# Reordering one core's three-block network: first-layer front, attention heads one by one, feed-forward fronts, and GpSimd's queue

## The reference

```
rkv = einsum(xs[:3], w_rkv);  r, k, v = rkv
decay = exp(-exp(w_log));  a = sigmoid(a0 + (xa @ a1) @ a2);  g = sigmoid(xg @ g1) @ g2
kk = (k * k_k) / max(norm(k * k_k), 1e-12)
k = k * (1.0 + (a - 1.0) * k_a)
S_t = S_{t-1} * w_t + (S_{t-1} @ -kk_t) (kk_t * a_t)^T + v_t k_t^T;  y_t = S_t @ r_t
yn = (y - mean) * rsqrt(var + LNX_EPS) * lnx_w + lnx_b
bonus = sum(r * k * r_k) * v;  out = ((yn + bonus) * g) @ w_o
MLA: q, k from latents, 32 of 96 columns rotated; softmax(q k^T + mask) v, 16 heads
conv_ffn: gate, up = x @ w_in;  h = gelu(conv(gate)) * up;  h @ w_out
```

## Time and profile before

| | |
|---|---|
| median of 3 runs | 1089.64 us (1087.91, 1089.64, 1090.89) |
| the profiled execution's own time | 1084.79 us |
| its span | 1083.0 us |
| mean granted clock of TensorE | 0.997 |
| busy: TensorE, VectorE, ScalarE, GpSimd | 1060.6, 791.5, 611.5, 219.0 us |
| chain that ended last | TensorE 77%, VectorE 12%, DMA 3%, issue 2%, ScalarE 2%, GpSimd 2% |

### The profile page before, as it was taken

One profiled execution on the slowest core, in us unless ns is written; L12 is line 12 of the kernel. 1 busy time (PEld: TensorE's weight loads), 2 busy tenths in 40 slices (PEclk: granted clock), 3 DMA queues, 4 the chain that ended last, 5 costly groups with the idle time before them and its releaser, 6 DMA issues.

```text
span 1083.0 us, 18718 instructions
## 1 busy us (share of the span) xinstructions
PE 1060.6 (98%) x7143; PEld 915.8 (85%) x7143; DVE 791.5 (73%) x1092; ACT 611.5 (56%) x965; POOL 219.0 (20%) x234
## 2 busy tenths in 40 slices
PE   7999999999999999999999999999999999999997
PEld 6997798888888898789888888998777889888886
DVE  7997867878885568777888666688868776666543
ACT  6766276656664576855666454645665446555531
POOL 0125483122220011001222100561100001112200
PEclk9999999999999999999999999999999999999999
DMA  8553172657767466455766674556552654666552
GB/s 247 171 174 123 40 231 84 176 156 195 192 195 264 149 146 172 122 134 142 194 189 167 228 260 135 184 176 206 160 149 67 199 172 128 186 190 193 194 194 78
DMA packets 219748, 183.12 MB, mean 169 GB/s; under 512 B 43265, under 2 KB 197614, under 8 KB 219678
## 3 DMA queue, kind: packets, MB, share of 16 engines
q1 hardware_dynamic: 215710, 171.43, 53.0%
q0 software_dynamic: 3392, 8.66, 2.5%
q10 hardware_dynamic: 576, 2.07, 0.5%
HBM read 179.44 MB, written 2.69 MB: 168 GB/s over the span
## 4 chain that ended last, share of the span: by engine, by line
PE 77%; DVE 12%; DMA 3%; issue 2%; ACT 2%; POOL 2%; SPq 1%; DVEq 0%; POOLq 0%; ACTq 0%
PE bank L288 21%; PE bank L282 13%; PE bank L284 12%; PE bank L283 12%; PE bank L289 10%; DVE ring L417 3%; PE bank L1252 2%; DVE arena L1710 1%; PE bank L295 1%; DVE arena L1805 1%; DVE stat L1803 1%; PE bank L375 1%; PE bank L2182 1%; DMA arena<-in_kv_w_up 1%; SPq L3418 1%
## 5 line engine op out<-in xcount | busy, mean ns | idle before, releaser
L417 DVE TENSOR_TENSOR ring<-ring,arena 128x2048 fp32r<-128x2048 f32 (+1 forms) x138 | 311.1, 2258 | 112.0 <-ACT arena L411 110.3
L282 PE MATMUL bank<-arena 128*128 128x512 f32 (+3 forms) x980 | 343.8, 351 | 1.8 <-DVE ring L417 1.1
L288 PE MATMUL bank<-arena 128*128 128x512 f32 x960 | 333.6, 394 | 0.0
L411 ACT ACTIVATE arena<-ring 128x2048 fp32r<-128x2048 f32 (+1 forms) x145 | 272.3, 1880 | 95.7 <-DMA ring<-in_ffn_w_out 42.9
L289 PE MATMUL bank<-arena,ring 128*128 128x256 f32 x960 | 266.0, 277 | 0.0
L284 PE MATMUL bank<-arena 128*128 128x512 f32 (+3 forms) x720 | 264.8, 368 | 0.0
L283 PE MATMUL bank<-ring,arena 128*128 128x512 f32 (+2 forms) x560 | 216.1, 386 | 0.0
L288 PEld LDWEIGHTS bank<-arena 128*128 128x128 f32 x960 | 180.0, 188 | 41.5
L282 PEld LDWEIGHTS bank<-arena 128*128 128x128 f32 x980 | 185.4, 189 | 26.9 <-issue 4.1
L289 PEld LDWEIGHTS bank<-arena,ring 128*128 128x128 f32 x960 | 180.3, 188 | 0.0
L284 PEld LDWEIGHTS bank<-arena 128*128 128x128 f32 x720 | 135.6, 188 | 22.4
(11 more groups left out here) (338 smaller groups left out, 1273.8 us busy)
## 6 DMA issues: line engine op xcount, KB each, us to landing
ring<-in_ffn_w_in SPq DMA_DIRECT2D x80, 512.0 KB, 5.0
ring<-in_ffn_w_out SPq DMA_DIRECT2D x44, 512.0 KB, 4.4
ring<-in_w_gate_up SPq DMA_DIRECT2D x40, 512.0 KB, 5.0
ring<-in_w_in SPq DMA_DIRECT2D x18, 1024.0 KB, 5.1
ring<-in_a_w_rkv SPq DMA_DIRECT2D x12, 1024.0 KB, 5.6
ring<-in_w_down SPq DMA_DIRECT2D x22, 512.0 KB, 3.7
ring<-in_a_w_o SPq DMA_DIRECT2D x4, 1024.0 KB, 7.1
arena<-in_ffn_w_in SPq DMA_DIRECT2D x8, 512.0 KB, 4.9
```

What stands on the lines that cost most here:

```text
L282: nc.tensor.matmul(dst, stationary[0], moving[0], start=start, stop=False)
L288: nc.tensor.matmul(dst[:, :], stationary[0], both_parts, start=start, stop=False)
L411: nc.scalar.activation(buf(hi_of(n), 0, w, arena12), ring[:, r, 0:w], ACT.Copy).then_inc(hi_ready, 1)
L417: on.tensor_tensor(ring12[:, r, 0:w], ring[:, r, 0:w], buf(hi_of(n), 0, w, arena12).bitcast(F32), ALU.subtract).then_inc(split_ready, 1)
```

## The change

On ScalarE, the split of the second half of the k input goes behind the two evacuations of the lora products; (a-1)k_a + 1 is made there by eight activations in place of L1757, with a small `key_bias` = 1 - k_a from VectorE, so that the new keys become a plain product; the spread of the second norms comes before the third exponential. On VectorE, three splits of weights and both key_maxima stand earlier, and the last split of w_r stands ahead of the first removal matrix. bonus_sums(1) goes from the products of v to a place between the pair banks, and into bank 0. SP loads the late inverse blocks ahead of w_o's first and second slot. GpSimd's second mask waits for the substitution, and its two parameter loads go behind the last mask and both saves of y. In the feed-forward fronts xn_turns of the second half stands before early_turn(0, 0), and eight padding products are gone; in the first front early_lo(0, 0) moves into the output stage of the time mix. In MLA the heads go one by one on all three engines. The core of the diff (the rest are the same moves on the engines that answer):

```diff
             early(0, 0)
             early(1, 0)
+            xn_turns(pe, i - 1, 1)
             early_turn(0, 0)
-            xn_turns(pe, i - 1, 1)
             early_turn(1, 0)
-            keep_busy(pe, 4, 2)
             early(0, 1)
...
             if f != 1:
-                early_lo(dve, f, 0 if f == 0 else 1)
+                early_lo(dve, f, 1)
             turn_dve(dve, turn, 0, 4, hi, lo)
-            if f == 0:
-                early_lo(dve, f, 1)
...
             gated_out(1, 1)
             o_lo(1, 0)
+            early_lo(dve, 0, 0)
             o_lo(1, 1)
...
-                if s == 2:
-                    pe.wait_ge(tok_evac, 4)
-                    bonus_sums(1)
-
-            pe.wait_ge(bonus_copied, NT)
+
+            pe.wait_ge(bonus_copied, 1)
             pe.wait_ge(tok_evac, 4)
             for l in range(PAIR_BANKS):
+                if l == 4:
+                    pe.wait_ge(v_evac, 1)
+                    bonus_sums(1)
...
             xs_split_act(act, "k", 0)
-            xs_split_act(act, "k", 1)
             after_slots(act, "lora_wa")
...
             nc.scalar.activation(lora[64:P, 0:T], bank[3][64:P, 0:T], ACT.Copy).then_inc(lora_hidden, 1)
+            xs_split_act(act, "k", 1)
...
             ahead(act, FIRST["w_r"] + 1, split_act)
+            act.wait_ge(kk_ready, 1)
+            for c in range(DC):
+                op = nc.scalar.activation(chan(W_T1)[:, c, :], chan(W_A)[:, c, :], ACT.Identity, scale=col("a_k_a", c),
+                                          bias=key_bias[:, c:c + 1])
+            op.then_inc(iclr_sig, 1)
             keys_out(3)
...
+            key_maxima(1)
             ahead(dve, FIRST["w_r"] + 1, split_dve)
 
-            dve.wait_ge(mix_done, MIXED["v"])
-            dve.wait_ge(iclr_sig, 4)
-            for c in range(DC):
-                op = nc.vector.tensor_scalar(chan(W_T1)[:, c, :], aT[:, c, :], 1.0, col("a_k_a", c), ALU.subtract, ALU.mult)
-            link(dve, op)
-            key_maxima(1)
+            dve.wait_ge(iclr_sig, 5)
             dve.wait_ge(k_evac, 4)
...
             pool.wait_ge(prod_evac, PAIR_BANKS)
+            pool.wait_ge(solved, 1)
             read_masked(W_RB[1])
             pool.wait_ge(prod_evac, PAIR_BANKS + PAIR_BANKS // NT)
             read_masked(W_RK[0])
-            pool.wait_ge(prod_mm, PAIR_BANKS)
-            pool.dma_start(buf(W_LNX, 0, D), A["a_lnx_w"][0].partition_broadcast(P)).then_inc(lnx_landed, 16)
-            pool.dma_start(buf(W_LNX, D, 2 * D), A["a_lnx_b"][0].partition_broadcast(P)).then_inc(lnx_landed, 16)
...
             read_masked(W_RK[1])
-            pool.wait_ge(y_saved, 16)
+            pool.wait_ge(prod_mm, PAIR_BANKS)
+            pool.wait_ge(y_saved, 32)
+            pool.dma_start(buf(W_LNX, D, 2 * D), A["a_lnx_b"][0].partition_broadcast(P)).then_inc(lnx_landed, 16)
+            pool.dma_start(buf(W_LNX, 0, D), A["a_lnx_w"][0].partition_broadcast(P)).then_inc(lnx_landed, 16)
             pool.wait_ge(solved, 2)
...
-            for h in range(4, H, 2):
-                for x in range(2):
-                    turn_p(h + x)
-                    if h + 2 < H:
-                        scores(h + 2 + x)
-                for x in range(2):
-                    values(h - 2 + x)
-                if h == 4:
+            for h in range(4, H):
+                turn_p(h)
+                if h + 2 < H:
+                    scores(h + 2)
+                if h == 6:
                     swapped(3)
-                if h == 12:
+                values(h - 2)
+                if h == 13:
                     o_turns(0)
-            for x in range(2):
-                values(H - 2 + x)
+            values(H - 2)
+            values(H - 1)
...
             rwkv_inverse_sp(sp)
+            rwkv_inverse_late_sp(sp, 0)
             rows_of("w_o", A["a_w_o"][0], 2, range(0, 1))
-            rwkv_inverse_late_sp(sp, 0)
+            rwkv_inverse_late_sp(sp, 1)
             rows_of("w_o", A["a_w_o"][0], 2, range(1, 2))
-            rwkv_inverse_late_sp(sp, 1)
```

More of the change, by code:

```diff
@@ L1108, in build @@
         head_gain = small(2 * DC)
+        key_bias = small(DC)
         bon, y_sum, y_sq, y_var, y_rstd = (small(32) for _ in range(5))
@@ L1295, in bonus_sums @@
                 for c in range(DC):
-                    if a == 1 and c == 4:
-                        keep_busy(pe, 1, 7)
-                    mm = by_columns(bank[6][:, a * H + 2 * c:a * H + 2 * c + 2],
+                    mm = by_columns(bank[(6, 0)[a]][:, a * H + 2 * c:a * H + 2 * c + 2],
                                     chan(W_K)[:, c, a * P:(a + 1) * P], head_gain[:, 2 * c:2 * c + 2], True, True)
@@ L1421, in o_turn @@
                 mm.then_inc(o_mm, 1)
+            pe.wait_ge(bonus_copied, NT)
             pe.wait_ge(v_evac, 4)
@@ L1606, in rwkv_act @@
                 nc.scalar.activation(buf(W_TOK, j * HALF, (j + 1) * HALF), bank[4 + j][:, :], ACT.Copy).then_inc(tok_evac, 1)
-            act.wait_ge(bonus_summed, 2)
-            nc.scalar.activation(bon[:, H:2 * H], bank[6][:, H:2 * H], ACT.Copy).then_inc(bonus_copied, 1)
             act.wait_ge(tok_mm, 5)
@@ L1613, in rwkv_act @@
                 nc.scalar.activation(buf(W_V, j * HALF, (j + 1) * HALF), bank[j][:, :], ACT.Copy).then_inc(v_evac, 1)
+            act.wait_ge(bonus_summed, 2)
+            nc.scalar.activation(bon[:, H:2 * H], bank[0][:, H:2 * H], ACT.Copy).then_inc(bonus_copied, 1)
             for l in range(PAIR_BANKS):
@@ L1721, in rwkv_dve @@
             xs_split_lo(dve, nc.vector, "r")
+            ahead(dve, FIRST["w_k"] + 2, split_dve)
             mixed("g")
-            ahead(dve, FIRST["w_k"] + 2, split_dve)
             mixed("v")
+            nc.vector.tensor_scalar(key_bias, cols[:, COL["a_k_a"]:COL["a_k_a"] + DC], -1.0, 1.0, ALU.mult,
+                                    ALU.add).then_inc(kk_ready, 1)
             kT, kk, sig, cum, aT = chan(W_K), chan(W_KK), chan(W_SIG), chan(W_CUM), chan(W_A)
@@ L1730, in rwkv_dve, with key_maxima @@
                                     spread(const("head_of").unsqueeze(1), [P, DC, 2]), ALU.mult)
+            def key_maxima(hf):
+                dve.wait_ge(kk_summed, hf + 1)
+                nc.vector.tensor_scalar(kk_inv[:, hf * H:(hf + 1) * H], bank[2 * hf][:, 0:H], 1e-24, None,
+                                        ALU.max).then_inc(var_ready, 1)
+            ahead(dve, LAST["w_k"], split_dve)
             dve.wait_ge(decay_sig, 4)
@@ L1736, in rwkv_dve @@
                 if c == 3:
-                    ahead(dve, LAST["w_k"], split_dve)
+                    key_maxima(0)
+                    ahead(dve, FIRST["w_r"], split_dve)
             link(dve, op)
-            def key_maxima(hf):
-                dve.wait_ge(kk_summed, hf + 1)
-                nc.vector.tensor_scalar(kk_inv[:, hf * H:(hf + 1) * H], bank[2 * hf][:, 0:H], 1e-24, None,
-                                        ALU.max).then_inc(var_ready, 1)
-            key_maxima(0)
-            ahead(dve, FIRST["w_r"], split_dve)
             tiles = buf(W_CUM).rearrange("p (n t) -> p n t", t=P)
@@ L2230, in mla_pe @@
             scores(3)
-            values(0)
             q_rope(3)
             turn_p(2)
+            values(0)
             swapped(2)
@@ L2365, in mla_act @@
             evac(1)
[L2366 removed]
+            split_act_half(act, o_w + 1, 0)
             q_rotary(3)
@@ L2373, in mla_act @@
             exps(5)
-            for h in range(4, H - 2, 2):
+            for h in range(4, H - 2):
                 evac(h)
-                if h == 6:
+                if h == 12:
                     split_act_half(act, o_w + 1, 1)
-                evac(h + 1)
                 exps(h + 2)
-                exps(h + 3)
             o_hi(0)
@@ L2508, in mla_dve @@
             q_odd_heads(1)
-            roped(0)
+            sined(0)
+            for h in range(4):
+                roped(h)
             maxima(0)
@@ L2512, in mla_dve @@
             maxima(1)
-            roped(1)
+            sined(1)
+            for h in range(4, 8):
+                roped(h)
             maxima(2)
@@ L2516, in mla_dve @@
             o_w = FIRST["o_w"]
+            split_half(dve, o_w, 0)
             maxima(3)
-            split_half(dve, o_w, 0)
-            maxima(4)
-            maxima(5)
-            roped(2, range(0, 2))
-            maxima(6)
-            maxima(7)
-            roped(2, range(2, 4))
             split_half(dve, o_w, 1)
-            for h in range(8, H):
+            sined(2)
+            for h in range(4, 8):
                 maxima(h)
-                if h == 9:
-                    roped(3, range(0, 2))
-                if h == 11:
-                    roped(3, range(2, 4))
-                if h == 13:
-                    normalized(0)
+                roped(h + 4)
+            maxima(8)
+            sined(3)
+            roped(12)
+            for h in range(9, 12):
+                maxima(h)
+                roped(h + 4)
+            maxima(12)
```

(4 more changed lines are left out.)

37 lines of the change are left out of this document (18 added, 19 removed).

## The result

| | median | runs | ratio to before, 95% interval |
|---|---|---|---|
| before | 1089.60 us | 1087.91 to 1090.89, 4 runs | |
| changed | 1096.44 us | 1094.77 to 1098.96, 4 runs | 1.0070 [1.0044, 1.0096] |
| forecast | 1086.4 us | 1082.5 to 1090.0 | |

The change makes the kernel 6.8 us slower. The prediction had it 3.2 us faster, and the time lies outside its range, on the side to which it gave 5 chances in 100. The profiled execution of the changed kernel took 1094.77 us, with a span of 1093.0.

What follows compares the result with a forecast made beforehand. TensorE, busy 98% of the span, was taken as the bound, so only its gaps and side work could be won. Terms 0.0 - 1.5 - 0.5 - 0.3 - 0.9 = -3.2 us gave 1086.4 us, range 1082.5 to 1090.0.

Steps and rivals of the forecast that it cites:

- the landing of the parameter loads: First layer, GpSimd: second load lands 5.5 us after issue, at 148.6; GpSimd's idle time absorbs the delay, term 0.0.
- The late-landing rival: GpSimd's parameter loads take 10.4 us, first rest 4.5 us later, clock falls: +2.6 in sum, 1092.2 us; chance 0.10.
- the first term: First feed-forward front: early_lo moved, turns' wait and padding gone, one new wait of 0.5: -1.5 us.
- the main case: After the substitution wait, the clock still falls to its lower level, costing 1.3 us as before.
- the forecast 0.6: First layer, TensorE: one new wait of 0.6 us for the split of w_r+1, now behind the maxima.
- that paragraph: First layer up to the substitution: VectorE's chain and TensorE each gain 1.8 us, so the substitution ends 1.8 earlier.
- so 0.0: SP's inverse blocks ahead of two w_o loads: the splits of w_o have slack, costing nothing.
- the term of -0.3: Ahead of attention: a ScalarE square moved before the weights' high part releases the third L282 wait, -0.3 us.
- the term had -0.9: Attention heads one by one: 2.0 us of waits go, switches cost 1.1 (0.22 a pair), net -0.9 us.
- All three signs of being wrong: Landing beyond 6 us, clock below 1.0 anywhere but after the substitution, or a pair of heads over 3.2 us.
- a rival at 0.17: After the substitution the clock does not fall, saving 1.3 us in the pairs: 1085.1 us; chance 0.17.
- The other rival on the clock: Clock falls in the new, nearly 2 us TensorE wait before 172.52, costing 1.3: 1087.7 us; chance 0.07.

Runs made afterwards that it cites:

- after: The changed kernel as first profiled, all of the change against the kernel before: 1096.44 us, ratio 1.0070; its profiled execution took 1094.77 us.
- after_again: The changed kernel, unchanged, profiled a second time: 1095.50 us, ratio 1.0090 to the kernel before.
- b_lnx_new: The kernel before with only the two parameter loads moved behind the last mask and both saves of y: 1092.96 us, ratio 1.0074.
- a_front_back: The changed kernel with TensorE's feed-forward fronts as before, turns' order and padding products both back: 1091.36 us, ratio 1.0031 to the kernel before.
- a_pad_back: The changed kernel with only the eight padding products back in each front: 1095.51 us, ratio 1.0067 to the kernel before.
- a_lnx_mid: The changed kernel with TensorE's fronts as before and the parameter loads one mask earlier, ahead of the last mask: 1084.76 us, ratio 0.9968 to the kernel before.
- a_lnx_front_back: The changed kernel with both the parameter loads and TensorE's feed-forward fronts as before: 1083.50 us, ratio 0.9969 to the kernel before.
- a_lnx_back: The changed kernel with GpSimd's two parameter loads back behind the second mask, ahead of the centred values: 1090.44 us, ratio 1.0023 to the kernel before.

## Why the prediction was wrong, point by point

**The step that failed is the landing of the parameter loads**, which the prediction put at 5.5 us for the second load, with a term of 0.0. It measured 8.6, 8.8 and 9.1 us in after, after_again and b_lnx_new (8.7 and 8.1 in a_front_back and a_pad_back). The reasoning was that the save of y, their neighbour before, would be gone. The save did profit: it took 2.6 us in the changed kernel instead of 6.2. But with it SP ran ahead, and its next load of 1 MB for w_o went out at 139.32, 1.5 us in front of the parameter loads; before, it went out at 138.07, behind them. In the 2.9 us after the first parameter load was issued SP's queue moved 0.97 MB, which kept the DMA engines busy for 84% of the time, and no packet of the parameters moved; in b_lnx_new it is 1.01 MB in 4.0 us. Their first packet came 1.3 us after the issue in the kernel before and in a_lnx_mid. This order of the two loads is read from the traces; no run moved the w_o load alone. The prediction held against the rival that both landed "with the same neighbours"; they had not, since the w_o load stood behind them then.

The price behind the landing was low too. GpSimd's rest (4.30 in place of 2.36) now met a split on VectorE, which the sum did not have, and the TensorE waits brought a fall of the clock, which it had in rivals only. The late-landing rival had the mechanism and the sign, at 1092.2; I gave it 0.10 because the two rows of before spoke against it. They were measured with other neighbours, and should have been the low end of the range rather than its middle. (Its own sum put 10.4 in the place of 5.9, where the forecast has 5.5, and so is 0.4 short.) In times, the move costs 8.0 us in the kernel before (1.0074) and 6.7 in the changed one (1.0031 against 0.9969).

**The second is a term that was not there**: the pace of the feed-forward loops. The sum gave the fronts 2.0 us of gain. In time TensorE's new fronts lose 2.4 us in the kernel before (1.0022) and 5.9 in the changed one (1.0023 against 0.9969). Locally the gain exists: from the first turn to the loop's first L288 the first front takes 17.5 us in the changed kernel against 19.0 before (forecast -1.5), the second and third 17.5 against 17.7 (forecast -0.25 each, measured -0.2). Most of the first term is VectorE's early_lo, though: with TensorE's front as before (a_lnx_front_back) it is 17.7. The loss is 2.1 us in each loop that is slow: two more slow loops in three, as the counts have it, would make 4.2 us less the 0.6 that TensorE's three fronts gain, which lies between the two measured times.

**What held, and what only seemed to.** The wait for the substitution ended at 125.08 (forecast 125.0), 1.7 earlier than before, and was 2.1 us long (1.9 before). In after_again, where the clock fell as the main case had it, the loads went out at 142.59 and 143.19 (forecast 142.5 and 143.1). The waits at L1208 and of L282 on the splits up to 45 us are gone. A new wait of 0.5 stands at L295, the size of the forecast 0.6, but it is for ScalarE's squares of the keys and not for the split of w_r: that match is luck. (TensorE's gains in that paragraph, 0.6, 0.8 and 0.7 less 0.6, sum to 1.5 and not 1.8; what set the end of the wait was VectorE's chain.)

The 1.7 us last through the first layer only in part or not at all, even without the late loads: the first turns of the first front start at 195.65 in a_lnx_back and 194.34 in a_lnx_front_back (194.3 to 197.4 in the six such profiles), against 195.63 before. The prediction said that the splits of w_o have slack, "so 0.0"; the rows under a_lnx_back show a wait there, of 1.5 and 0.4 us on TensorE in these two. No run put SP's order back alone.

In attention, the term of -0.3 was misplaced: the third wait of L282 on a split is at 873.8 us, in the second block, and it is still there (0.38 before and after). The heads themselves, from the first turned head to the first product of the output weights, take 29.6 us in all ten profiles of the new order and 30.1 in all five of the old, -0.5 where the term had -0.9. Both its parts can be seen. TensorE's timeline in the changed kernel:

```profile
451.18 0.57 PE L295 MATMUL bank<-arena 128*64 128x64 f32 x12
451.68 0.55 PE L2195 MATMUL bank<-cst,arena 128*128 128x128 f32 x3
452.07 0.82 PE L2186 MATMUL bank<-arena 98*128 98x128 f32 x4
452.82 0.57 PE L295 MATMUL bank<-arena 128*64 128x64 f32 x12
```

No row waits, and a head takes 452.82 - 451.18 = 1.64 us, 3.28 for a pair, where two heads by twos took 3.0. The prediction charged 0.22 a pair for the switches; it is 0.3. Of the 2.0 us of waits, 0.5 stayed (0.3 at the scores, 0.2 at a turn). All three signs of being wrong came true: a landing beyond 6 us, a clock below 1.0 in another place, and a pair of heads over 3.2 us.

**The clock.** That it would fall behind the substitution was the main case, that it would not a rival at 0.17. It fell in 13 of the 15 profiles, after_again among them, and not in the first profile of the changed kernel nor in b_lnx_new, whose TensorE program is that of the kernel before. The wait was 1.8 to 2.1 us in all of them. So it differs between executions of one kernel, and is not a result of the change. Where it falls it costs 1.7 us, and not 1.3. The other rival on the clock, a fall in the new wait near 172.52, came true as well: 0.82 from 173 to 176 and 0.71 behind it.

## What to carry to other kernels

A load that is moved next to its reader needs a bound from the worst landing that the new neighbours allow, not from its own row at the old place. Moving it also sets its old neighbours free, and what they release may go out in front of it. Here the move turned a free load into 7 us of waiting, and one mask earlier (4.5 us) made it free again. Count what runs beside the work that is delayed too, since a late engine meets instructions that it used to miss. And where a kernel's unrelated loops change by 2%, profile the unchanged kernel a second time before looking for a cause in the diff.

## What the runs showed of the hardware that was not expected

The same stream of matmuls, with no wait in it and a granted clock of 1.00, runs in one of two steady paces that last through a whole loop of 111 us: 346.6 or 353.3 ns for a pair of 512 and 256 columns. TensorE's timeline of the kernel before:

```profile
299.89 0.40 PE L288 MATMUL bank<-arena 128*128 128x512 f32 x1
300.12 0.28 PE L289 MATMUL bank<-arena,ring 128*128 128x256 f32 x1
300.24 0.39 PE L288 MATMUL bank<-arena 128*128 128x512 f32 x1
300.47 0.27 PE L289 MATMUL bank<-arena,ring 128*128 128x256 f32 x1
```

and of the changed kernel:

```profile
299.83 0.40 PE L288 MATMUL bank<-arena 128*128 128x512 f32 x1
300.07 0.28 PE L289 MATMUL bank<-arena,ring 128*128 128x256 f32 x1
300.18 0.40 PE L288 MATMUL bank<-arena 128*128 128x512 f32 x1
300.42 0.28 PE L289 MATMUL bank<-arena,ring 128*128 128x256 f32 x1
```

The starts are 0.23 us apart from L288 to L289 in the first, 0.24 in the second. By exact starts the quick pace repeats after two pairs and the slow one after three, in which two intervals are 5 to 10 ns longer. Both occur in one execution of one kernel.

A rest on GpSimd and a split on VectorE, each with two inputs from on-chip memory, do not run side by side: the one that starts second stands until the first has ended, and the first is not slowed. In the changed kernel the split started at 150.96 inside the first rest, which kept its 2.36 us and ended at 152.47; the split took 3.66 instead of 2.28 and ended at 154.62; the second rest, started at 152.54, took 4.30 instead of 2.36. In after_again the split started first, at 151.78, and kept its 2.28 us; the rest that started at 152.04 took 4.25. The profiles of a_front_back, a_pad_back and b_lnx_new fit the same reading. The Trainium skill, GPSIMD Engine Reference (1. Specifications), says that the two engines share their interfaces to this memory, with contention when VectorE's instruction has two such inputs; the trace agrees, and gives it 1.9 us for one pair of instructions.
